# Input projection in token blocks of 384/384/320, taps begun on the first 768 tokens, convolution shared out anew, the sample's LayerNorm apart

## The reference, cut to what matters

```
h = rms_norm(x, norm1_g);  z = h @ w_in                  # 1024 -> 1536: pool 512, value 512, gate 512
y_pool = (trailing mean over 2/4/8/16 - token) @ pool_lin[g] * pool_scale
v = value * sigmoid(gate)
c = depthwise causal conv(v, width 31) + bias            # prompt and sample have prefixes of their own
y_conv = silu(layer_norm(c) * ln_g + ln_b)               # LayerNorm over the 512 channels
x = x + concat(y_pool, y_conv) @ w_out + b_out
x = x + hier_moe(rms_norm(x, norm2_g))                   # best group of 4, best 2 experts of its 8
y = rms_norm(x, norm_f_g)
```

## Time and profile before

| | us |
|---|---|
| median of 3 runs | 1068.87 |
| lowest, highest | 1068.7, 1072.86 |
| the profiled execution, its own time | 1070.19 |
| its span in the trace | 1068.4 |
| busy PE, DVE, ACT, POOL | 945.7, 865.0, 635.7, 293.1 |

### The profile page before, as it was taken

How to read it: one execution, slowest core, us unless ns; L and a number is a source line. 1 busy time by engine, 2 the same in 40 slices (tenths; PEclk the granted TensorE clock), 3 DMA queues, 4 the chain that set the end, 5 groups by cost and what they waited for, 6 DMA issues and landing times.

```text
span 1068.4 us, 13431 instructions
## 1 busy us (share of the span) xinstructions
PE 945.7 (89%) x4446; PEld 774.7 (73%) x4446; DVE 865.0 (81%) x967; ACT 635.7 (59%) x623; POOL 293.1 (27%) x324
## 2 busy tenths in 40 slices
PE   4999999896898783969999999999999999999920
PEld 3888888574687563758888888888888888888720
DVE  6289998969756646889889898989898989898658
ACT  7244453563531103648787878787878787878515
POOL 2178688375153101002121212121212121212010
PEclk8999999897998875879999999999999999999965
DMA  8221111121351142579999999999999999999877
GB/s 265 82 61 40 40 40 45 37 104 45 133 217 60 69 153 90 214 262 368 379 377 390 389 391 383 402 384 384 384 392 372 384 384 374 380 385 384 296 248 273
DMA packets 67531, 268.63 MB, mean 251 GB/s; under 512 B 15359, under 2 KB 28159, under 8 KB 42921
## 3 DMA queue, kind: packets, MB, share of 16 engines
q1 hardware_dynamic: 57993, 250.36, 63.0%
q0 software_dynamic: 9504, 17.85, 4.4%
HBM read 254.09 MB, written 30.86 MB: 267 GB/s over the span
## 4 chain that ended last, share of the span: by engine, by line
PE 84%; DVE 6%; ACT 3%; DMA 3%; issue 3%; POOL 1%; SPq 0%; DVEq 0%; POOLq 0%; ACTq 0%
PE ps L1076 11%; PE ps L1074 11%; PE ps L1075 11%; PE ps L925 8%; PE ps L1088 6%; PE ps L1090 6%; PE ps L1089 6%; PE ps L801 5%; PE ps L802 5%; PE ps L803 5%; PE ps L1063 3%; PE ps L980 2%; PE ps L1095 1%; PE ps L839 1%; DMA arena<-hm_scratch,g_idx 1%
## 5 line engine op out<-in xcount | busy, mean ns | idle before, releaser
L726 ACT ACTIVATE big<-arena 128x2048 fp32r<-128x2048 f32 x192 | 362.5, 1913 | 70.4 <-PE ps L1090 38.6
L1525 DVE TENSOR_TENSOR low<-arena,big 128x2048 fp32r<-128x2048 f32 x126 | 285.2, 2285 | 39.8 <-ACT big L726 39.8
L1074 PE MATMUL ps<-big,ring 128*128 128x512 f32 x512 | 204.4, 399 | 2.4 <-DVE ring L1530 2.4
L1076 PE MATMUL ps<-big,ring 128*128 128x512 f32 x512 | 202.4, 395 | 0.0
L1525 DVE TENSOR_TENSOR big<-arena,big 128x2048 fp32r<-128x2048 f32 x66 | 151.0, 2289 | 16.5 <-ACT big L726 16.2
L1208 DVE SCALAR_TENSOR_TENSOR ps<-arena,cols,ps 128x512 f32<-128x512 f32 (+1 forms) x174 | 137.2, 788 | 6.0
L925 PE MATMUL ps<-big,ring 128*128 128x512 f32 (+1 forms) x432 | 113.4, 423 | 14.0 <-DVE ring L1274 7.1
L1074 PEld LDWEIGHTS ps<-big,ring 128*128 128x128 f32 x512 | 96.9, 189 | 22.1 <-DVE ring L1530 2.8
L925 PEld LDWEIGHTS ps<-big,ring 128*128 128x128 f32 (+1 forms) x432 | 84.6, 199 | 38.6 <-DVE ring L1274 7.5
L1076 PEld LDWEIGHTS ps<-big,ring 128*128 128x128 f32 x512 | 96.9, 189 | 21.2
L1088 PE MATMUL ps<-big,hT 128*128 128x512 f32 x256 | 103.0, 402 | 10.1 <-DVE hT L1540 10.1
(11 more groups left out here) (240 smaller groups left out, 1394.7 us busy)
## 6 DMA issues: line engine op xcount, KB each, us to landing
arena<-in_w_eg SPq DMA_DIRECT2D x64, 1024.0 KB, 7.5
arena<-in_w_eu SPq DMA_DIRECT2D x64, 1024.0 KB, 7.2
arena<-in_w_ed SPq DMA_DIRECT2D x64, 1024.0 KB, 7.6
arena<-in_x_prompt SPq DMA_DIRECT2D x16, 512.0 KB, 4.5
y_in<-y_scratch SPq DMA_DIRECT2D x16, 512.0 KB, 7.8
arena<-in_w_in SPq DMA_DIRECT2D x12, 512.0 KB, 3.6
arena<-in_w_out SPq DMA_DIRECT2D x8, 512.0 KB, 3.9
x_scratch<-arena SPq DMA_DIRECT2D x8, 512.0 KB, 2.6
```

The source lines that it names most:

```text
L726: act.activation(we_h[n % RING], raw[n % RING], ACT.Copy).then_inc(high_done, 1)
L1074: pe.matmul(out, part_h[b][:, k, :], wh[:, q, :], start=(k == 0), stop=False)
L1076: ins = pe.matmul(out, part_l[b][:, k, :], wh[:, q, :], start=False, stop=(k == KD - 1))
L1525: dve.tensor_tensor(we_l[n % RING], raw[n % RING], we_h[n % RING].bitcast(F32), ALU.subtract).then_inc(low_done, 1)
```

## The change

Seven things change, all in the front part.

1. **Blocks.** `Z_BLOCKS` are 384, 384 and 320 tokens, each in a PSUM bank of its own. A chunk has still 72 matmuls. Bank 7 is no longer part of DVE's accumulator, and LayerNorm block 0 uses it.
2. **Start.** Weights 0 and 1 are loaded and split earlier. `in_proj(0, 0)` follows tile 3, `in_proj(1, 0)` tile 5, `in_proj(0, 1)` tile 7. Signals `z_early` and `sg_half` let ACT and DVE take the first 768 tokens of gate 0 and value 0 before the rest is made. POOL fills the convolution's borders earlier.
3. **DVE's taps.** Part B is now 512 wide (prompt only). DVE does A of all tiles and B of tiles 0 and 3. Six of the 31 taps of B of tile 0 are done before `glu(1)` and accumulate in `hc` in SBUF (`held`).
4. **Shares.** Share 0 is tile 1 (606 wide), shares 1 and 2 are 400 and 206 columns of tile 2. Share 3 is new: the 64 sample tokens of tiles 0 and 3 together (two ACT products of 64 columns and one POOL addition of 128 x 2 x 64 per tap).
5. **Where the shares stand.** Share 0 goes with steps 4 to 8, share 1 with steps 8 and 11 and the rest behind `ln_swish(0)`, share 2 between tiles 2 and 3 of the output projection, share 3 with 8 products behind `ln_square(1)` and 23 behind `row_deviation(3)`. On POOL all additions of share 3 stand before `mix_low(4)`.
6. **The sample's LayerNorm** is done apart: mean before and variance after `out_conv(5)`, `ln_swish(2)` before `mix_high(7)`.
7. **Orders.** `state_rows(0)` and `(1)` stand together before the products of step 9; the squares of block 0 are four instructions; DVE waits for share 3 before `route(0)`; the load of the first expert pieces is put off from tile 4 to tile 5.

```diff
+    ZB = 3 * P
+    Z_BLOCKS = [(0, ZB), (ZB, ZB), (2 * ZB, T - 2 * ZB)]
-        PART = {"A": (0, BANK), "B": (BANK, HW_)}
-        HELPED = [(0, BANK, HW_), (1, BANK, CUT), (1, CUT, HW_)]
-        help_n = {2: (0, 6), 3: (0, 7), 4: (0, 7), 5: (0, 7), 6: (0, 3), 7: (1, 10), 8: (1, 10), 9: (1, 10)}
+        PART = {"A": (0, BANK), "B": (BANK, SEQ)}
+        HELPED = [(1, BANK, HW_), (2, BANK, CUT), (2, CUT, HW_), (slice(0, NC, 3), HW_ - DEC, HW_)]
+        help_n = {4: ((0, 6),), 5: ((0, 7),), 6: ((0, 7),), 7: ((0, 7),), 8: ((0, 3), (1, 6)), 11: ((1, 6),)}
@@ ACT, in the loop over chunks
                 if j == 8:
                     state_rows(0)
-                if step_j in help_n:
-                    h, n = help_n[step_j]
-                    products(h, n + (made[h] == 0))
-                if j == 8:
                     state_rows(1)
                 if j == 10:
                     ln_square(0)
-            wo_high(0)
-            wo_high(1)
-            wo_high(2)
-            wo_high(3)
-            pooled(0)
+                for h, n in help_n.get(j + 1, ()):
+                    products(h, n + (made[h] == 0))
@@ ACT, after it
+            for k in range(NC):
+                wo_high(k)
             ln_swish(0)
             mix_conv_high(0)
+            products(1, 6)
+            pooled(0)
             pooled(1)
             mix_conv_high(1)
+            products(1, 4)
             state_rows(2)
             wo_high(4)
             wo_high(5)
+            products(1, 4)
             state_rows(3)
             wo_high(6)
             wo_high(7)
+            products(1, 4)
...
-            products(2, 14)
+            products(2, 4)
+            mix_high(2)
+            products(2, 8)
             row_deviation(0)
-            mix_high(2)
-            products(2, TAPS - 14)
+            products(2, 4)
+            mix_high(3)
+            products(2, 8)
             row_deviation(1)
-            mix_high(3)
+            products(2, TAPS - 24)
+            row_deviation(2)
+            hm_turned(0)
             ln_square(1)
-            ln_square(2)
-            hm_turned(0)
-            row_deviation(2)
+            products(3, 8)
             ln_deviation(1)
-            ln_deviation(2)
+            hm_turned(1)
             ln_swish(1)
-            ln_swish(2)
             mix_high(4)
             row_deviation(3)
-            hm_turned(1)
+            products(3, TAPS - 8)
             mix_high(5)
             hm_turned(2)
@@ PE
+            pe.wait_ge(help_done, 4 * TAPS)
+            pe.wait_ge(lnsd_done, 2)
+            ln_mean(2)
             out_conv(5)
+            ln_variance(2)
@@ DVE
+            glu_first(0)
+            taps(10, "A", 0)
+            glu_rest(0)
+            taps(TAPS - 10, "A", 0)
+            taps(6, "B", 0, 6)
             glu(1)
...
+            taps(10, "B", 0, 6)
             ln_center(0)
             difference(0)
+            taps(3, "B", 0, 6)
             difference(1)
+            taps(4, "B", 0, 6)
             difference(2)
             ln_normal(0)
...
+            mix_conv_low(2)
+            mix_pool_low(2)
+            pooled_sample()
+            taps(4, "B", 3)
+            residual(0)
+            taps(6, "B", 3)
+            hm_row(0)
+            residual(1)
+            mix_conv_low(3)
+            mix_pool_low(3)
+            taps(TAPS - 18, "B", 3)
...
+            dve.wait_ge(help_done, 4 * TAPS)
             route(0)
@@ POOL
+                if step_j >= 9:
+                    windows(POOL_ORDER[step_j - 9])
+                for h, n in help_n.get(step_j, ()):
+                    additions(h, n)
             windows(POOL_ORDER[3])
+            additions(1, 10)
+            wo_low(POOL_WO[0])
+            additions(1, 4)
+            wo_low(POOL_WO[1])
+            wo_low(POOL_WO[2])
+            additions(1, 4)
...
+            additions(2, 3)
+            bias(0)
+            bias(1)
+            additions(2, TAPS - 4)
+            bias(2)
+            bias(3)
+            additions(3, TAPS - 1)
+            for t in range(4, NT):
+                mix_low(t)
+                bias(t)
```

More of the change, by code:

```diff
@@ L562, in pool_in @@
                 act.wait_ge(z_done, j + 1)
[L563 to L569, removed]
+                first, rest = z_first[j % 2], z_rest[j % 2]
@@ new lines, in pool_in @@
+                act.activation(u_ext[:, g, PS:PS + 2 * ZB].rearrange("p (b n) -> p b n", b=2), first, ACT.Copy)
+                act.activation(u_ext[:, g, PS + 2 * ZB:PS + SEQ], rest[:, 0:Z_SEQ], ACT.Copy)
+                act.activation(u_end[:, g, 0, :], rest[:, Z_SEQ - PS:Z_SEQ], ACT.Copy)
+                act.activation(u_end[:, g, 1, :], rest[:, Z_SEQ + DEC - PS:Z_SEQ + DEC], ACT.Copy)
+                act.activation(u_ext[:, g, PS + SEQ + PS:UW], rest[:, Z_SEQ:Z_SEQ + DEC], ACT.Copy).then_inc(u_done, 1)
@@ L571, in products @@
+            made = [0, 0, 0, 0]
             def products(h, n):
                 c, a, b = HELPED[h]
+                tiles = range(NC)[c] if h == 3 else (c,)
                 if made[h] == 0:
-                    act.wait_ge(v_done, c + 1)
-                    if h:
+                    act.wait_ge(v_done, tiles[-1] + 1)
+                    if h == 1:
                         act.wait_ge(help_done, h * TAPS)
+                    elif h == 3:
+                        act.wait_ge(wl_done, NCH + len(POOL_WO))
@@ L578, in products @@
                 for j in range(made[h], made[h] + n):
[L579 to L587, removed]
+                    if j >= 4:
+                        act.wait_ge(help_done, h * TAPS + j - 2)
@@ new lines, in products @@
+                    for i, tile in enumerate(tiles):
+                        scale = cols[:, tile, j:j + 1]
+                        if j == 0:
+                            ins = act.activation(hc[:, tile, a:b], v_ext[:, tile, a:b], ACT.Identity, scale=scale,
+                                                 bias=cols[:, tile, R_B:R_B + 1])
+                        else:
+                            to = taps_pr[3 * max(h - 1, 0) + j % 3]
+                            ins = act.activation(to[:, i * (b - a):(i + 1) * (b - a)], v_ext[:, tile, a + j:b + j],
+                                                 ACT.Copy, scale=scale)
@@ L606, in ln_square @@
                 if n == 0:
-                    act.wait_ge(help_done, 2 * TAPS)
+                    for c in range(NC):
+                        act.activation(sq0[c], hc[:, c, 0:BANK], ACT.Square).then_inc(sq_done, 1)
+                    return
                 act.activation(sq[n][:, :, 0:w], hc[:, :, hc_at(tok):hc_at(tok) + w], ACT.Square).then_inc(sq_done, 1)
@@ new lines, in taps @@
+            def taps(n, part, c, held=0):
+                a, b = PART[part]
+                for _ in range(n):
+                    j = at_tap.get((part, c), 0)
+                    own = hc[:, c, a:b]
+                    to = own if j == TAPS - 1 or j < held else acc_ps
+                    run = own if j <= held else acc_ps
+                    dve.wait_ge(conv_step, steps[0] if j in (0, held) else last[part, c])
+                    if j == 0:
+                        if part == "B":
+                            dve.wait_ge(v_done, c + 1)
+                        dve.tensor_scalar(to, v_ext[:, c, a:b], cols[:, c, 0:1], cols[:, c, R_B:R_B + 1], ALU.mult,
+                                          ALU.add).then_inc(conv_step, 1)
+                    else:
+                        dve.scalar_tensor_tensor(to, v_ext[:, c, a + j:b + j], cols[:, c, j:j + 1], run, ALU.mult,
+                                                 ALU.add).then_inc(conv_step, 1)
+                    steps[0] += 1
+                    at_tap[part, c], last[part, c] = j + 1, steps[0]
```

230 lines of the change are left out of this document (114 added, 116 removed).

## The result

The changed kernel takes 1085.64 us (median; 1085.33 to 1086.66), the kernel before 1070.8 us in the same session. The ratio is 1.0137, with a 95% interval of 1.0108 to 1.0167: slower by some 15 us. The forecast was 1085 in a range of 1063 to 1096, and slower with a chance of 0.76.

A forecast was written before the change was run, and what follows sets the result against it. Three times decide: projection's end, last tap and out_conv(4), after which PE, DVE and ACT alternate without slack. 1070.2 - 6.1 + 17.9 + 4.5 = 1086.5, the median 1.3 lower: 1085 us, range 1063 to 1096.

The forecast's parts named there:

- The projection's price: PE's projection: 384- and 320-column matmuls pay by the column, chunk 11.7 to 11.8 us instead of 13.68, 23 us for twelve.
- The start: Up to part A's end: first matmul 20.7, first 768 tokens at 43, glu(1) 73.7, conv_done 1 at 152 to 153.
- The six held taps: DVE's taps before glu(1) with running sum in SBUF: no extra cost while POOL idles, otherwise 2 us.
- POOL and ACT fall behind: Projection: share 0 starts at 75, ends at 134; PE idles 5.5 us in chunk 9; projection ends about 183, 18 earlier.
- the 2.8 us for a low clock: PE in chunk 9: after its idle time, matmuls run at first at the lower clock, adding 2.8 us.
- The forecast's terms for the projection's end: 51 + 10 x 11.7 + transposes 0.9 + mean and variance of block 0 6.9 + 8.3 = about 183.
- Share 1 in the mix of block 0: POOL's last 18 additions and three wo_low end at 225, delaying low halves to 226; last tap 258.5, 6 us earlier.
- its bound without the two waits: Last tap at 251 without PE's idle time in chunk 9 and the wait of ln_deviation(0).
- Share 2's term: POOL beside DVE's last taps: 2 x 2.6 for bias and 30 x 0.685, ending at 254.
- The wait for share 3: Before out_conv(4): 23 POOL additions at 0.55 us precede mix_low(4); out_conv(4) at 306.3, +47.8 after the last tap.
- the 18 between +47.8 and +29.9: Last tap to out_conv(4): forecast +47.8 us against 29.9 in the kernel before, 18 more.
- The tail: From out_conv(4) on: lower clock +1.2, sample's mean and variance +2, table loads +1.3, together +4.5; residual(5) at 342.

The follow-up runs named there:

- slow chunks: Changed kernel with 13 extra matmuls of 320 columns per projection chunk from the third on: 1099.34 us; same edit on the old shares: 1080.65 us.
- share 3 late: Changed kernel with the last 23 products of share 3 behind mix_high(5) and their additions behind mix_low(4), bias(4) and mix_low(5): 1080.03 us.
- share 1 light: Changed kernel with taps 13 to 30 of share 1 made on 4 columns only, all waits kept: 1080.11 us.
- share 3 spread: Changed kernel with share 3's products split 8, 12 and 11 over ACT's gaps, additions spread likewise, first route waiting for share 2 only: 1074.78 us.
- the old tiles at the new places: Changed kernel with share 3 spread, but tiles shared out as before the change, nothing held, additions at the changed kernel's places: 1076.63 us.
- the old places: Changed kernel with convolution work shared and placed nearly as before the change, blocks and early begin kept: 1060.49 us, or 1055.48 us with share 3 spread.
- the old shares: Changed kernel with the convolution shared out and ordered nearly as before the change; blocks, early begin and separate sample LayerNorm kept: 1060.49 us.
- the best version: The old shares, with share 3's products made 8, 12 and 11 at a time in ACT's gaps: 1055.48 us, ratio 0.9857.
- old shares, slow chunk: The old shares with 13 further matmuls of 320 columns per projection chunk from the third on: 1080.65 us, ratio 1.0106.

## Why the prediction was right

**The projection's price** held: matmuls of 384 columns start 0.173 us apart and those of 320 columns 0.147, so a chunk takes 11.84 us (11.7 to 11.8 forecast). That this reaches the end is shown by the two runs with slow chunks.

**The start** was 1 to 3 us off: the first matmul at 22.0 (20.7), the first product of gate and value at 45.2 (43), `glu(1)` at 76.7 (73.7), part A's end at 154.1 (152 to 153). The delay on DVE at `glu(1)` was 1.05 us, which the forecast did not have.

**The six held taps** cost nothing extra, as forecast: 3.90 us for five with the sum in SBUF, 0.78 each, where the earlier trace rows have 0.79 with it in PSUM. The Trainium skill says of the shared SBUF interfaces that DVE's instructions with two SBUF inputs contend there (GPSIMD Engine Reference, "1. Specifications"); POOL was idle beside these taps, so no run here shows what they would cost next to it.

**POOL and ACT fall behind**: right in kind, too large in size. Share 0 ended at 134.9 (134), but PE stood for 2.61 us (5.5), and its granted clock was 1.00 from 143 to 151 us, so the 2.8 us for a low clock did not come. That was partly luck. The runs with share 3 late, share 1 light and share 3 spread are the same up to there and wait 2.56 to 2.61 us. In the first two the clock stayed up as well; in the third it was 0.54 from 143 to 146, and its chunk 9 took 16.58 us instead of 15.15:

```profile
143.57 1.03 PE L864 MATMUL ps<-ident,arena 128*30 128x128 f32 x4 [2.61 <-ACT arena L615]
```

The forecast's terms for the projection's end add up to 184.1, not 183. Chunk 2 began at 52.6, 1.6 later than the 51 in that sum, ten chunks took 1.4 more, and wait and clock 5.7 less: 181.4, where 181.8 was measured. Errors of both signs are thus why the middle came out right: `ln_deviation(0)` at 184.6 (184), the high half of tile 0 at 194.6 (196).

**Share 1 in the mix of block 0**: its end at 225.1 (225), the low halves done at 225.7 (226), the last tap at 259.2 (258.5), and share 2's end at 259.5 (254). That this stretch costs is shown by share 1 made light; that the orders cost and not the tiles, by the old tiles at the new places. The prediction had POOL's late start, but mis-sized what it costs: its bound without the two waits was a last tap at 251, and with the old places it came at 242, 17 us sooner. Share 2's term was mis-sized too: its 206-column additions took 0.88 us each in the last piece (16.78 for 19) instead of 0.685, waits for ACT included. The mean of block 1 waited for it and not for the last tap, which the forecast did not have. It ended only 0.3 us behind the last tap, so this miss did not show.

**The wait for share 3**: 17 us of POOL idle, then 23 additions in 13.05 us, 0.567 each (0.55), `out_conv(4)` at 307.8 (306.3), 48.6 after the last tap (47.8; the forecast's terms, 33.4, 12.6 and 1.2, add up to 47.2). That it goes away when share 3 is placed otherwise is shown by four runs (late, spread, and the old shares with and without spreading). Spreading it is worth 10.9 us, not the 18 between +47.8 and +29.9. From the mean to `out_conv(4)` it took 33.9 instead of 48.2 us, 14.3 less. The mean itself came 1.9 later in that run, mostly from the lower clock in chunk 9, and the profiled executions differ by 13.2 us where the medians differ by 10.9. Only in the run with share 3 late did the chain of row tiles take much of the gain back.

**The tail**: from `out_conv(4)` to the end it is 777.0 us of the span against 773.9, so +3.1 where +4.5 was forecast. `residual(5)` came at 342.6 (342). With share 3 spread it is 776.0, and 777.7 in the best version, so 2 to 4 us of it stay without that wait for share 3 and also with the old shares.

So 1085 was right by its steps, with errors of 1 to 6 us that cancel in part. That the separate LayerNorm of the sample is what costs the 3 us of the tail was not tried by itself.

**Where 15 us of loss come from.** Blocks: -13.7. Early begin: -7.9. The shares' new places: +19.3. Share 3 before `mix_low(4)`: +10.9. The tail: +3.1. These are each one edit against a neighbour and need not add up; they come to +11.7 where +14.8 was measured. They depend on what they are tried on: with the old shares the blocks bring 17 to 20 us and the early begin 3.4.

## What to carry to other kernels

When a stage gets shorter, look at what ran under its cover: here POOL began its additions 24 us later than it could (80.2 against 56.1) and did that work later, where DVE and PE had to wait for it. A helper's work belongs in the earliest stretch in which its input is there, and work with a late deadline must not stand ahead of work with an early one on any queue, nor may it be moved to where a third engine's small step waits behind it. A wait removed is worth only what the chain behind it can use: 17 us at `out_conv(4)` gave 5.6.

## What the runs showed of the hardware that was not expected

POOL's 606-column additions took 1.55 us each in the earlier trace rows and in the five runs here whose share 0 is tile 0 (10.86 to 10.88 us for seven in the later sets), but 1.45 in the changed kernel and the five runs in which it is tile 1 (10.13 to 10.17), with the same shape and DVE at its 512-column taps beside them. What makes the difference was not tried.

After idle time PE's 24 matmuls of 512 columns took 7.2 to 8.3 us instead of 5.75, and the length of the wait does not order them. They took 7.37 after 3.26 us (old shares) and 8.04 after the same 3.26 (old shares, slow chunk), 8.34 after 3.63, 7.99 after 10.03 (both with share 3 spread) and 8.08 after 23.92 (changed kernel). Behind waits of 1.4 to 2.0 us they took 5.74 to 5.79.

```profile
226.41 8.34 PE L962 MATMUL ps<-big,ring 128*128 128x512 f32 x24 [3.63 <-DVE ring L1338]
```

So a wait of 3 to 4 us costs 1.4 to 2.6 us on top of itself in these runs, and one of 24 us 2.0 to 2.5. From 308 to 316 us of the changed kernel, where `out_conv(4)` runs after its wait, the granted clock was 0.70, so part of it ran at the lower level. The 2.61 us of waiting in chunk 9 cost nothing on top in the changed kernel and 1.4 us in the run with share 3 spread.
